# Reordering the steps of a chunked gated delta rule on one core: solve by direction, correction and across product a step ahead, the state product in two halves

## The reference

```
def step(state, inp):
    q_i, k_i, u_i, w_i, a_i, g_i = inp
    v_new = u_i - einsum('bhcd,bhdv->bhcv', w_i, state)
    o = (einsum('bhcd,bhdv->bhcv', q_i * exp(g_i)[..., None], state)
         + einsum('bhce,bhev->bhcv', a_i, v_new))
    g_last = g_i[..., -1]
    state = (state * exp(g_last)[..., None, None]
             + einsum('bhcd,bhcv->bhdv', k_i * exp(g_last[..., None] - g_i)[..., None], v_new))
    return state, o
```

## Time and profile before

| | |
|---|---|
| median of 3 runs | 2392.94 us (2383.0 to 2394.9) |
| profiled execution | 2387.24 us, span 2385.6 us |
| mean granted clock over the span | 0.973 |
| delta phase, first to last step | 997 to 1169 us of the span |

### The profile page before, as it was taken

How to read it: one execution, slowest core, us unless ns; L and a number is a source line. 1 busy time by engine, 2 the same in 40 slices (tenths; PEclk the granted TensorE clock), 3 DMA queues, 4 the chain that set the end, 5 groups by cost and what they waited for, 6 DMA issues and landing times. The chain is left out here.

```text
span 2385.6 us, 44710 instructions
## 1 busy us (share of the span) xinstructions
PE 2241.1 (94%) x18162; PEld 1977.9 (83%) x18162; DVE 1433.4 (60%) x1812; ACT 1069.7 (45%) x1581; POOL 522.2 (22%) x562
## 2 busy tenths in 40 slices
PE   6999999999999998788889999799999999999996
PEld 5777788999899986687635555799999999999995
DVE  6555412145565658455464578677777777777776
ACT  4666411011111148312365533466666666666665
POOL 1000000012767937534331200010000001000001
PEclk9999999999999999989789999899999999999998
DMA  3233422348788868789644413677777778877766
GB/s 126 77 108 92 145 86 91 111 117 232 213 227 225 208 197 263 188 229 249 196 157 144 140 54 138 235 271 277 255 273 264 267 247 275 274 261 268 265 220 210
DMA packets 267870, 469.84 MB, mean 197 GB/s; under 512 B 152208, under 2 KB 192784, under 8 KB 240560
## 3 DMA queue, kind: packets, MB, share of 16 engines
q1 hardware_dynamic: 232688, 411.62, 53.2%
q0 software_dynamic: 13856, 48.32, 7.1%
q10 hardware_dynamic: 21152, 7.48, 1.4%
HBM read 363.77 MB, written 107.49 MB: 198 GB/s over the span
## 5 line engine op out<-in xcount | busy, mean ns | idle before, releaser
L78 DVE TENSOR_TENSOR ex_w_rest<-weights,ex_w_rounded 128x2048 fp32r<-128x2048 f32 x192 | 439.4, 2290 | 203.6 <-ACT ex_w_rounded L2804 201.8
L2804 ACT CAST ex_w_rounded<-weights 128x2048 fp32r<-128x2048 f32 x192 | 365.7, 1905 | 12.4 <-PEq L48 12.4
L2696 PE MATMUL ex_g_acc<-ex_xt,ex_w_rounded 128*128 128x320 f32 x1024 | 270.7, 347 | 2.1 <-ACT ex_xt L2816 2.1
L2696 PE MATMUL ex_u_acc<-ex_xt,ex_w_rounded 128*128 128x320 f32 x1024 | 270.1, 347 | 0.0
L2697 PE MATMUL ex_g_acc<-ex_xt,ex_w_rest 128*128 128x160 f32 x1024 | 242.3, 237 | 0.0
L2697 PE MATMUL ex_u_acc<-ex_xt,ex_w_rest 128*128 128x160 f32 x1024 | 241.4, 236 | 0.0
L2697 PEld LDWEIGHTS ex_g_acc<-ex_xt,ex_w_rest 128*128 128x128 f32 x1024 | 196.9, 192 | 0.0
L2697 PEld LDWEIGHTS ex_u_acc<-ex_xt,ex_w_rest 128*128 128x128 f32 x1024 | 195.6, 191 | 0.0
L2696 PEld LDWEIGHTS ex_g_acc<-ex_xt,ex_w_rounded 128*128 128x128 f32 x1024 | 193.3, 189 | 2.5 <-issue 2.5
L2696 PEld LDWEIGHTS ex_u_acc<-ex_xt,ex_w_rounded 128*128 128x128 f32 x1024 | 192.0, 188 | 0.2
L2670 POOL DMA_INDIRECT x<-ex_ys,rt_sample_idx x15 | 24.5, 1634 | 638.8 <-issue 471.1
(11 more groups left out here) (418 smaller groups left out, 5208.6 us busy)
## 6 DMA issues: line engine op xcount, KB each, us to landing
weights<-in_w_expert SPq DMA_DIRECT2D x192, 1024.0 KB, 4.9
tk_w<-in_w_tok SPq DMA_DIRECT2D x10, 1344.0 KB, 7.6
ch_w<-in_w_ch SPq DMA_DIRECT2D x24, 512.0 KB, 5.7
sc_rows<-rows SPq DMA_DIRECT2D x40, 256.0 KB, 6.3
sc_qk<-qkv_ch SPq DMA_DIRECT2D x40, 256.0 KB, 6.4
laq<-sc_laq SPq DMA_DIRECT2D x80, 128.0 KB, 4.4
dl_kv<-qkv_tok SPq DMA_DIRECT2D x40, 256.0 KB, 4.1
dl_kq<-laq SPq DMA_DIRECT2D x20, 512.0 KB, 5.0
```

The source lines that it names most:

```text
L78: return dve.tensor_tensor(out, whole, rounded.bitcast(F32), ALU.subtract)
L2696: pe.matmul(bank[:, 0:2 * SLOTS], hi[:, cols], x.rearrange("p a n -> p (a n)"), start=first, stop=False, skip_group_check=True)
L2804: act.copy(w_hi[:, i % SPLIT], held[:, i % HELD]).then_inc(w_rounded, 1)
```

## The change

- `solve` no longer calls `product`: it does the eight heads of direction 0 as soon as that direction's `r` is there, then the eight of direction 1.
- `from_state` is cut in two: the keys' half (64 columns, its own semaphore `ks_done`, for which `remainder` now waits), then `queries`, the other half. 16 products become 32.
- `correction(s+1)` moves from behind `solve(s)` to ahead of it, and `across` is done two steps ahead instead of one, behind it. `masked` on DVE follows `across`.
- The copy `vb` is split: heads 0 to 3 by ACT, heads 4 to 7 by DVE (`values`).
- DVE's order becomes `keep(s)`, `remainder(s)`, `values(s)`, `masked(s+2)`, `carried(s)`, `transposed(s+1)`.
- `off` and `x0` count on a semaphore of their own (`across_in`, 4 loads) and are loaded five steps ahead; the other six loads stay three ahead, in a slightly other order, and `correction` waits for them.

```
 LOADED_EARLY = 2
-LOADS = 10
+LOADS = 6
+ACROSS_LOADS = 4
...
+ACROSS_AHEAD = RING + 1
...
+                for s in range(AHEAD_STEPS, ACROSS_AHEAD):
+                    across_blocks(s)
                 for p in range(STEPS):
+                    if p + ACROSS_AHEAD < STEPS:
+                        across_blocks(p + ACROSS_AHEAD)
                     s = p + AHEAD_STEPS
                     if s < STEPS:
                         b = s % RING
                         sp.wait_ge(kq_done, p + 1)
-                        sp.wait_ge(lx_done, p + 1)
-                        load_across(sp, dr, off[b], x0[b], loaded[b], s)
-                        sp.wait_ge(lx_done, p + 2)
                         tokens(s, 0)
+                        sp.wait_ge(corrected, p + 2)
+                        tokens(s, 1)
                         sp.wait_ge(v_done, p + 1)
-                        tokens(s, 1)
-                        sp.wait_ge(corrected, p + 2)
                         load_keys_queries(sp, dr, kq[b], loaded[b], s)
...
-                            mm = pe.matmul(uobank[:, b % 2, d, h, :], kq[b][rows, h, :], state[rows, h, :], start=(h == 0), stop=False, skip_group_check=True)
+                            mm = pe.matmul(uobank[halves[d], b % 2, d, h, :], kq[b][rows, h, halves[d]], state[rows, h, :], start=(h == 0), stop=False, skip_group_check=True)
+                    mm.then_inc(ks_done, 1)
+
+                def queries(s, b):
+                    for h in range(NH):
+                        for d, rows in enumerate(halves):
+                            mm = pe.matmul(uobank[halves[1 - d], b % 2, d, h, :], kq[b][rows, h, halves[1 - d]], state[rows, h, :], start=(h == 0), stop=False, skip_group_check=True)
                     mm.then_inc(kq_done, 1)
...
-                    pe.wait_ge(r_out, 2 * s + 2)
...
-                    product(vbank, xt[:, b], r, v_done)
+                    for d, rows in enumerate(halves):
+                        pe.wait_ge(r_out, 2 * s + 1 + d)
+                        passed(s)
+                        for h in range(NH):
+                            mm = pe.matmul(vbank[rows, h // 4, h % 4, :], xt[rows, b, h, :], r[rows, h, :], start=True, stop=True)
+                    mm.then_inc(v_done, 1)
...
                     from_state(s, b)
-                    if more:
-                        across(s + 1, nb, ni)
+                    queries(s, b)
+                    if not last(s, 1):
+                        correction(s + 1, (b + 1) % RING, i + (b + 1) // RING)
+                    if not last(s, 2):
+                        across(s + 2, (b + 2) % RING, i + (b + 2) // RING)
                     solve(s, b)
-                    if more:
-                        correction(s + 1, nb)
                     to_state(s, b)
                     to_output(s, b)
...
-                    act.copy(paired(vb[:]), vbank).then_inc(v_out, 1)
+                    act.copy(vb[:, 0:4], vbank[:, 0]).then_inc(v_low_out, 1)
...
+                def values(s):
+                    dve.wait_ge(v_done, s + 1)
+                    dve.tensor_copy(vb[:, 4:8], vbank[:, 1]).then_inc(v_high_out, 1)
+
                 def step(s, b, i, prompt):
-                    more = not (isinstance(s, int) and s == STEPS - 1)
-                    nb = (b + 1) % RING
+                    keep(s, b)
                     remainder(s, b)
-                    if more:
-                        masked(s + 1, nb)
-                    keep(s, b)
-                    if more:
-                        transposed(s + 1, nb)
-                    else:
+                    values(s)
+                    if not last(s, 2):
+                        masked(s + 2, (b + 2) % RING)
+                    if last(s, 1):
                         first_tile.statistics(dve)
                     carried(s, b)
+                    if not last(s, 1):
+                        transposed(s + 1, (b + 1) % RING)
```

More of the change, by code:

```diff
@@ L1445, with last @@
 RING = 4
+def last(s, count):
+    return isinstance(s, int) and s >= STEPS - count
 def ring_steps(engine, body):
@@ L1513 @@
     loaded: list
+    across_in: list
     CONSTANTS = 16 * 4
@@ L1520, in start @@
             load_columns(engine, dr, self.cols, self.const_in)
-        load_across(engine, dr, self.off[s], self.x0[s], self.loaded[s], s)
+        load_across(engine, dr, self.off[s], self.x0[s], self.across_in[s], s)
         load_inverse(engine, dr, self.x1[s], self.loaded[s], s)
@@ L1534, in early_loads @@
     cols = sb("dl_cols", [P, STEPS, 5, NH])
-    return EarlyLoads(**of, cols=cols, spread=spread, const_in=nc.alloc_semaphore("dl_const_in"), loaded=[nc.alloc_semaphore(f"dl_loaded{b}") for b in range(LOADED_EARLY)])
+    return EarlyLoads(**of, cols=cols, spread=spread, const_in=nc.alloc_semaphore("dl_const_in"), loaded=[nc.alloc_semaphore(f"dl_loaded{b}") for b in range(LOADED_EARLY)],
+                      across_in=[nc.alloc_semaphore(f"dl_across_in{b}") for b in range(LOADED_EARLY)])
 AHEAD_STEPS = RING - 1
+ACROSS_AHEAD = RING + 1
 MIXER_STEPS = (4, 7, 10, 13)
@@ L1569, in phase_delta @@
         loaded = [*begun.loaded, *(sem(f"dl_loaded{b}") for b in range(LOADED_EARLY, RING))]
+        across_in = [*begun.across_in, *(sem(f"dl_across_in{b}") for b in range(LOADED_EARLY, RING))]
         stored = [sem(f"dl_stored{b}") for b in range(2)]
         xt_ready, rhs_ready, prepared = sem("dl_xt_ready"), sem("dl_rhs_ready"), sem("dl_prepared")
-        lx_done, corrected, kq_done, v_done, kd_done, at_done = (sem(f"dl_{n}_done") for n in ("lx", "corrected", "kq", "v", "kd", "at"))
-        prod_out, xt_out, r_out, kept_out, v_out, o_out = (sem(f"dl_{n}_out") for n in ("prod", "xt", "r", "kept", "v", "o"))
+        lx_done, corrected, ks_done, kq_done, v_done, kd_done, at_done = (sem(f"dl_{n}_done") for n in ("lx", "corrected", "ks", "kq", "v", "kd", "at"))
+        prod_out, xt_out, r_out, kept_out, v_low_out, v_high_out, o_out = (sem(f"dl_{n}_out") for n in ("prod", "xt", "r", "kept", "v_low", "v_high", "o"))
         state_out, cleared = sem("dl_state_out"), sem("dl_state_cleared")
@@ L1584, in tokens, with across_blocks @@
                     load_tokens(sp, dr, kv[s % RING], loaded[s % RING], s, d)
+                def across_blocks(s):
+                    if s >= RING:
+                        sp.wait_ge(lx_done, s - RING + 1)
+                    load_across(sp, dr, off[s % RING], x0[s % RING], across_in[s % RING], s)
                 for s in range(LOADED_EARLY, AHEAD_STEPS):
-                    load_across(sp, dr, off[s], x0[s], loaded[s], s)
+                    across_blocks(s)
                     load_inverse(sp, dr, x1[s], loaded[s], s)
@@ L1673, in from_state @@
                         for d, rows in enumerate(halves):
-                            mm = pe.matmul(uobank[:, b % 2, d, h, :], kq[b][rows, h, :], state[rows, h, :], start=(h == 0), stop=False, skip_group_check=True)
+                            mm = pe.matmul(uobank[halves[d], b % 2, d, h, :], kq[b][rows, h, halves[d]], state[rows, h, :], start=(h == 0), stop=False, skip_group_check=True)
[4 more added lines that the diff above has]
+                            mm = pe.matmul(uobank[halves[1 - d], b % 2, d, h, :], kq[b][rows, h, halves[1 - d]], state[rows, h, :], start=(h == 0), stop=False, skip_group_check=True)
                     mm.then_inc(kq_done, 1)
                 def across(s, b, i):
-                    pe.wait_ge(loaded[b], 16 * LOADS * (i + 1))
+                    pe.wait_ge(across_in[b], 16 * ACROSS_LOADS * (i + 1))
                     if not early(s, 1):
@@ L1688, in solve, with correction @@
                     pe.wait_ge(xt_out, 2 * s + 2)
-                    pe.wait_ge(r_out, 2 * s + 2)
                     if not early(s, 1):
-                        pe.wait_ge(v_out, s)
-                    passed(s)
-                    product(vbank, xt[:, b], r, v_done)
-                def correction(s, b):
+                        pe.wait_ge(v_low_out, s)
+                        pe.wait_ge(v_high_out, s)
+                    for d, rows in enumerate(halves):
[4 more added lines that the diff above has]
+                    mm.then_inc(v_done, 1)
+                def correction(s, b, i):
+                    pe.wait_ge(loaded[b], 16 * LOADS * (i + 1))
                     pe.wait_ge(prod_out, 2 * s + 2)
@@ L1705, in to_state @@
                 def to_state(s, b):
-                    pe.wait_ge(v_out, s + 1)
+                    pe.wait_ge(v_low_out, s + 1)
+                    pe.wait_ge(v_high_out, s + 1)
                     pe.wait_ge(prepared, s + 1)
@@ L1721, in step @@
                 def step(s, b, i, prompt):
-                    more = not (isinstance(s, int) and s == STEPS - 1)
-                    nb, ni = (b + 1) % RING, i + (b + 1) // RING
                     from_state(s, b)
-                    if more:
-                        across(s + 1, nb, ni)
+                    queries(s, b)
```

(27 more changed lines are left out.)

## The result

The changed kernel takes 2418.62 us (median of 4 runs, 2412.97 to 2423.25), beside 2390.78 for the kernel before on the same chip: a ratio of 1.0136, 95% interval 1.0105 to 1.0167. The forecast was 2382 with a range up to 2404, so the time lies outside it and on the other side. The profiled execution took 2418.33, 31.1 more than that of before.

What follows compares the result with a forecast made beforehand. The bound was a closed state-to-state chain of 7.58 us a step, plus time at 1.2 GHz. Terms of +1.3 at 2.4 GHz and -12.5 for the clock gave -11.2 from the median 2392.94: 2382 us, range 2364 to 2404.

Steps and rivals of the forecast that it cites:

- rival F: Little happens: waits for loads or instructions, with a sixth more on TensorE, take back 6 us; 2388 us, chance 0.07.
- The clock, −12.5: TensorE's clock in the delta phase: filling the gap ahead of the solve wins back three quarters of 17 us.
- as before, 0: Middle bound for the clock in the delta phase: it falls as before, gaining 0 us.
- Rival C: TensorE's clock falls in most steps, low for 60% of 157 us: +26 us, 2419; chance 0.14.
- thin stretch: Correction, across, solve of one quarter at a time and waiting for the copy: 3.8 us a step, against 0.69 + 0.93.
- The step at 2.4 GHz: One delta-phase step at full clock: -0.59 + 0.86 - 0.16 = +0.11 us, a period of 7.7 us.
- Solve by direction: Solve on TensorE, sixteen records in one quarter, then sixteen in another: 2.01 us instead of 1.15, +0.86 a step.
- D: Solve records in one place are as fast as alternating ones: solve 1.15 us, 16 us less, 2366; chance 0.09.
- rival E: Solve's weight loads within one direction aren't hidden: 0.117 a record, solve 3.9 us, +37 us in all, 2431; chance 0.04.
- Loads, 0 to 2: Loads in the delta phase, asked for in a new order: cost 0, with up to 2 us at the start.

Runs made afterwards that it cites:

- the half split: Changed kernel with the state product in two halves only for heads 4 to 7, heads 0 to 3 whole: 2396.15 us, 1.0035.
- the changed kernel written out: Changed kernel with every step written out on TensorE instead of a loop, no backward branch: 2400.16 us, 1.0049.
- half of the across product twice: Kernel before, with half of the across product repeated in each step into the same place: 2390.84 us, 1.0014.
- the shifted half split: Kernel before with the state product split for heads 4 to 7 only, and eight more warm-up products ahead of the phase: 2381.62 us, 0.9982.
- the alternating solve: Changed kernel with the solve alternating between the directions again, nothing else undone: 2416.75 us, 1.0105.

## Why the prediction was wrong

**The step that failed** is a cost that the sum doesn't contain. "A sixth more [instructions] on TensorE" stands in rival F alone, with 6 us and a chance of 0.07, and its evidence was the earlier trace rows, a single wait; the sum puts waits for instructions at nothing. Measured, a loop fetched anew against one kept is 1.0136 against 1.0035 for the half split, 24 us, though that is not quite the same work; where only the place differs, 1.0097 against 0.9982, 27 us, and 1.0062 against 1.0006, 13 us; and 21 us against the changed kernel written out. I had the row and read it as a fault of step 1. What I didn't read is the instruction queue pass by pass, which showed before the change that passes 2 and 3 fetch nothing, thus that the loop lived on being kept.

Of its size, the waits at the branches in the changed kernel's trace are 3.81 + 1.95 and 3.80 + 1.22, 10.8 us. All waits for "issue" of half a microsecond and more are 25.0, against 2.0 before, which is most of the 31; the others lie within steps (2.15 at 1052, 1.80 at 1150) and behind the loop (3.03). Work at 1.2 GHz behind the waits, and loads (below), come on top. I didn't separate these by a run.

**The clock, −12.5: not delivered.** The half split in the changed kernel has the loop kept and no gap ahead of the solve, and its granted clock over the phase is no better than the 0.85 of the earlier trace rows:

```profile
997.00:1169.00 172.00, 151.22 (x3979) 142.26 (x3980) 96.41 (x173) 27.91 (x55) 71.97 (x63) 0.86 0.85 219
```

Choosing three quarters of the bound from what the falls have in common was wrong; "as before, 0" was near. The gap is not what decides: filled (here) and cut to 0.67 (half of the across product twice) it left 0.86 and 0.85, and the one profiled execution with 0.92, the shifted half split, has a gap of 0.63 in most steps. Why the falls persist is open.

**Rival C** gave the right time, 2419, for a wrong reason. It needed the clock low for 60% of the phase; 0.82 is 36%, and taking away the solve's part of the thin stretch it names (the alternating solve) changed less than the intervals resolve, while a lengthened across product with the old solve cost as much.

**The step at 2.4 GHz: right.** Predicted period 7.7, against 7.58 before. The changed kernel's first two state adds, with no wait between them, are 7.67 apart, in DVE's timeline:

```profile
1003.69 0.69 DVE L1829 TENSOR_TENSOR dl_state<-dl_vsbank,dl_kept 128x512 f32<-128x512 f32 x1 [0.58 <-PE dl_vsbank L1677]
1011.36 0.69 DVE L1829 TENSOR_TENSOR dl_state<-dl_vsbank,dl_kept 128x512 f32<-128x512 f32 x1 [0.38 <-PE dl_vsbank L1677]
```

Three of the half split, with the loop kept:

```profile
1083.87 0.69 DVE L1832 TENSOR_TENSOR dl_state<-dl_vsbank,dl_kept 128x512 f32<-128x512 f32 x1 [0.39 <-PE dl_vsbank L1677]
1091.49 0.69 DVE L1832 TENSOR_TENSOR dl_state<-dl_vsbank,dl_kept 128x512 f32<-128x512 f32 x1 [0.39 <-PE dl_vsbank L1677]
1099.19 0.69 DVE L1832 TENSOR_TENSOR dl_state<-dl_vsbank,dl_kept 128x512 f32<-128x512 f32 x1 [0.39 <-PE dl_vsbank L1677]
```

7.62 and 7.70. **Solve by direction**, 2.01: measured 1.90, so D and E are out. The Trainium skill ("TensorE: Matmul & The Clock Gate", "What overlaps and what doesn't") has a weight load overlap running matmuls only if its row group is another one. The measurement doesn't contradict that: 32 records, 16 of them in a row in one quarter, took 1.90, or 0.059 each, and alternating ones 1.15, or 0.036. What was wrong is rival E's price: it took the whole 0.117 of a twice as large record for one of half the size, where 0.059 is half of it. Whether the load is hidden in either can't be told from these rows.

**Loads, 0 to 2: too low.** In the changed kernel the correction product of an early step waits for them, in TensorE's timeline:

```profile
1017.43 0.90 PE L1729 MATMUL dl_ybank<-dl_x,dl_prod 32*32 32x32 f32 x26 [3.38 <-DMA dl_at<-laq]
```

and with the half split it waits 1.29 and 2.72 for `dl_x` in steps 15 and 18, 4.0 together. That, and the missing 12.5 of the clock, would make 16.5 of the 19.6 between the forecast (−11.2) and the half split (1.0035, +8.4). With the loop kept, none of the four forms of the change that ran was faster than before (1.0015, 1.0031, 1.0035, 1.0006), so the change would most likely not have been faster either.

## What to carry to other kernels

When a change lengthens a hardware loop, look in the trace at the instruction queue pass by pass. If passes after the first fetch nothing, the loop is being kept, and the added instructions have a price that is a step and not a slope: here nothing measurable for a loop of 1682 instructions, and 13 to 27 us for a loop of three passes at 1810 and more, or at 1682 and 1684 in another place. Moving the loop by a few harmless instructions ahead of it is a cheap test, and here it was worth 27 us to one kernel.

## What was not expected of the hardware

- A loop of 1554 to 1688 TensorE instructions was kept where it touched seven blocks of 256, and it, or a longer one (1810 to 1816), was fetched anew in each pass where it touched eight; thirteen loops agree, two of them forecast. The offset of the blocks is fitted, to within 32 instructions. The Trainium skill ("Runtime: NRT & Kernel Launch", "Instruction fetch mechanics") tells of 16 KiB blocks and a stall at a branch that leaves the fetched window, and both are seen here (packets of 16 KB, waits of 3.81 and 3.80); it also says that the prefetch is purely sequential and the window two pages, against which the second and third pass of the kernel before, a loop of more than six blocks, ran with no fetch at all.
- DVE's `keep`, beside POOL's preparation now, takes 0.69 to 1.66, a mean of 0.92 instead of 0.70 for the same tile. In the step at 1064 us, shown above, POOL's own product took 1.50 instead of 1.04 in the same moments. It lay in part under the state product; in the step where it took 1.66 the period was the 7.67 above.

The group of `keep` in the changed kernel (busy us, mean ns, idle before it):

```profile
L1824 DVE TENSOR_TENSOR dl_kept<-dl_state,dl_cols 128x512 f32<-128x512 f32 x20 | 18.4, 921 | 0.6
```
